# Sums of inner pieces made on GpSimd behind its own loads, in the second layer of a seven-product feed-forward

## What is computed

```python
hn = rms_norm(h, p['norm_ff_g'])
ff = jnp.square(jax.nn.relu(hn @ p['w_ff1'])) @ p['w_ff2']
return h + ff
```

## Time and profile before

| | us |
|---|---|
| median of 3 runs (lowest to highest) | 2295.55 (2292.86 to 2296.75) |
| profiled execution, its own time | 2294.14 |
| its span, first to last instruction | 2292.3 |
| TensorE busy / VectorE / ScalarE / GpSimd | 2216.3 / 1443.3 / 1068.5 / 166.5 |
| mean granted TensorE clock | 0.991 |

### The profile page before, as it was taken

How to read it: one execution, slowest core, us unless ns; L and a number is a source line. 1 busy time by engine, 2 the same in 40 slices (tenths; PEclk the granted TensorE clock), 3 DMA queues, 4 the chain that set the end, 5 groups by cost and what they waited for, 6 DMA issues and landing times.

```text
span 2292.3 us, 35228 instructions
## 1 busy us (share of the span) xinstructions
PE 2216.3 (97%) x13706; PEld 1996.7 (87%) x13706; DVE 1443.3 (63%) x2196; ACT 1068.5 (47%) x1870; POOL 166.5 (7%) x284
## 2 busy tenths in 40 slices
PE   8999999899998999999899999999999998899998
PEld 6888888788886888888688888999999998899998
DVE  6332455476654666677677554567677686766677
ACT  7533322265664444576634233465555643344432
POOL 0000000211100000000000000011111111111110
PEclk9999999999999999999999999999999999999999
DMA  5334322654546677888764344545546578887886
GB/s 167 108 110 138 119 93 74 164 137 131 146 122 173 227 231 242 254 260 269 248 234 125 89 160 144 175 162 197 205 161 222 168 274 307 260 253 245 271 308 212
DMA packets 227980, 434.92 MB, mean 190 GB/s; under 512 B 16355, under 2 KB 132963, under 8 KB 223116
## 3 DMA queue, kind: packets, MB, share of 16 engines
q1 hardware_dynamic: 188652, 321.71, 43.5%
q0 software_dynamic: 39200, 111.45, 15.6%
HBM read 331.93 MB, written 103.27 MB: 190 GB/s over the span
## 4 chain that ended last, share of the span: by engine, by line
PE 40%; DVE 7%; ACT 3%; issue 0%; DMA 0%; ACTq 0%; DVEq 0%
PE acc L148 11%; PE acc L150 11%; PE acc L149 11%; PE late_acc L148 2%; PE late_acc L149 2%; PE late_acc L150 2%; DVE w_lo L2535 2%; ACT ff_far_t_hi L2462 1%; DVE ff_far_t_lo L2540 1%; ACT w_hi L2465 1%; DVE ff_w_s L2589 1%; DVE ff_part_q L2593 1%; DVE ff_part_v L2593 1%; DVE t_lo L2540 1%; ACT t_hi L2462 1%
## 5 line engine op out<-in xcount | busy, mean ns | idle before, releaser
L148 PE MATMUL acc<-xn_hi,w_hi 128*128 128x512 f32 (+1 forms) x1176 | 420.6, 358 | 23.1 <-DVE xn_lo L617 10.0
L149 PE MATMUL acc<-xn_hi,w_lo 128*128 128x512 f32 (+1 forms) x1176 | 418.1, 356 | 0.0
L150 PE MATMUL acc<-xn_lo,w_hi 128*128 128x512 f32 (+1 forms) x1176 | 417.5, 355 | 0.0
L148 PE MATMUL late_acc<-xn_hi,w_hi 128*128 128x512 f32 (+1 forms) x768 | 285.9, 372 | 3.0 <-DVE late_result_a L867 1.9
L148 PEld LDWEIGHTS acc<-xn_hi,w_hi 128*128 128x128 f32 x1176 | 223.4, 190 | 58.1 <-issue 13.6
L150 PE MATMUL late_acc<-xn_lo,w_hi 128*128 128x512 f32 (+1 forms) x768 | 273.5, 356 | 0.0
L149 PE MATMUL late_acc<-xn_hi,w_lo 128*128 128x512 f32 (+1 forms) x768 | 272.8, 355 | 0.0
L150 PEld LDWEIGHTS acc<-xn_lo,w_hi 128*128 128x128 f32 x1176 | 223.2, 190 | 31.6
L149 PEld LDWEIGHTS acc<-xn_hi,w_lo 128*128 128x128 f32 x1176 | 223.4, 190 | 31.1
L149 PE MATMUL acc<-ff_far_t_hi,w_lo 128*128 128x320 f32 x804 | 249.7, 311 | 0.0
L148 PE MATMUL acc<-ff_far_t_hi,w_hi 128*128 128x320 f32 x540 | 168.4, 312 | 12.4 <-ACT hn_plain L2490 8.2
(11 more groups left out here) (312 smaller groups left out, 4609.4 us busy)
## 6 DMA issues: line engine op xcount, KB each, us to landing
w_raw<-in_w_tiles SPq DMA_DIRECT2D x82, 512.0 KB, 4.2
ff_w_s<-in_w_ff SPq DMA_DIRECT2D x64, 512.0 KB, 5.2
gates<-s_t_ops POOLq DMA_DIRECT2D x86, 320.0 KB, 3.6
ff_part_q<-s_u_T POOLq DMA_DIRECT2D x34, 640.0 KB, 5.9
c_w<-s_ac SPq DMA_DIRECT2D x20, 1024.0 KB, 5.0
ff_part_v<-s_u_T POOLq DMA_DIRECT2D x31, 640.0 KB, 5.5
s_late_T<-late_result_s SPq DMA_DIRECT2D x20, 640.0 KB, 7.1
ff_w_a<-in_w_ff SPq DMA_DIRECT2D x12, 1024.0 KB, 5.9
```

Source lines behind the costliest of these rows:

```text
L148: pe.matmul(out, w_hi, x_hi, start=first, stop=False, skip_group_check=onto)
L149: pe.matmul(out, w_lo, x_hi, start=False, stop=False, skip_group_check=onto)
L150: return pe.matmul(out, w_hi, x_lo, start=False, stop=last, skip_group_check=onto)
```

## The change

The sums of two inner pieces in the second layer are made by GpSimd instead of VectorE: behind the issue of the load for piece n, GpSimd waits for the load of piece n - 2 and adds its two pieces. VectorE keeps the sums of weights and makes them for the step after the next instead of the next, and in the second layer it makes the low half of the inner piece before that of the weights. Waits, counts and buffers are the same otherwise.

```diff
--- before.py
+++ after.py
@@ -2313,6 +2313,15 @@
                 at = self.INNER[i]
                 pool.wait_ge((out.even_out, out.odd_out, out.odd_out, out.mixed_out)[min(at, 3)], 16 * (k + 1))
             pool.dma_start(self.t_raw[s], self.t_ops[self.INNER[i], k]).then_inc(self.t_in[s], 16)
+
+        def add_pieces(n):
+            _, _, _, t, t_op, t_turned, _ = self.PRODUCTS[n // self.PAIRS]
+            r, H = n % self.RING, self.HALF
+            if len(t) == 2:
+                pool.wait_ge(self.t_in2[r], 16 * (n // self.RING + 1))
+                x, y = self.t_raw2[r][:, 0:H], self.t_raw2[r][:, H:2 * H]
+                pool.tensor_tensor(x, y if t_turned else x, x if t_turned else y, t_op).then_inc(self.t_sum2, 1)
+
         for n in range(self.STEPS - self.FIRST):
             p, r = n % self.PAIRS, n % self.RING
             pieces = self.PRODUCTS[n // self.PAIRS][3]
@@ -2334,6 +2343,10 @@
                 pool.dma_start(self.t_raw2[r].rearrange("p (q t) -> p q t", q=2), self.u_T[p, :, lo:hi + 1:hi - lo]).then_inc(self.t_in2[r], 16)
             else:
                 pool.dma_start(self.t_raw2[r][:, 0:self.HALF], self.u_T[p, :, pieces[0]]).then_inc(self.t_in2[r], 16)
+            if n >= 2:
+                add_pieces(n - 2)
+        for n in (self.STEPS - self.FIRST - 2, self.STEPS - self.FIRST - 1):
+            add_pieces(n)
 
     def sync(self, sp):
         ws, m, H, out = self.ws, self.m, self.HALF, self.out
@@ -2581,16 +2594,12 @@
             dve.scalar_tensor_tensor(at, at, 0.0, self.root[:, H * (q % 2):H * (q % 2 + 1)], ALU.max, ALU.mult).then_inc(self.relued, 1)
 
         def add_pieces(n):
-            w, w_op, w_turned, t, t_op, t_turned, _ = self.PRODUCTS[(n - self.FIRST) // self.PAIRS]
+            w, w_op, w_turned = self.PRODUCTS[(n - self.FIRST) // self.PAIRS][0:3]
             r, loaded = (n - self.FIRST) % self.RING, 16 * ((n - self.FIRST) // self.RING + 1)
             if len(w) == 2:
                 dve.wait_ge(self.w_in2[r], loaded)
                 x, y = self.w_raw2[r][:, 0:512], self.w_raw2[r][:, 512:1024]
                 dve.tensor_tensor(x, y if w_turned else x, x if w_turned else y, w_op).then_inc(self.w_sum2, 1)
-            if len(t) == 2:
-                dve.wait_ge(self.t_in2[r], loaded)
-                x, y = self.t_raw2[r][:, 0:H], self.t_raw2[r][:, H:2 * H]
-                dve.tensor_tensor(x, y if t_turned else x, x if t_turned else y, t_op).then_inc(self.t_sum2, 1)
 
         def add_result(p, c, f, of, cols):
             mh, th, op = self.PRODUCTS[p][6][c]
@@ -2619,12 +2628,12 @@
                     dve.tensor_tensor(self.a21[:, k], self.a11[:, k], self.a21[:, k], ALU.subtract).then_inc(self.s_sum, 1)
                 self.remainder_t(dve, n)
             else:
+                self.remainder_t(dve, n)
                 self.remainder_w(dve, n)
-                self.remainder_t(dve, n)
             if n == 3:
                 self.out.mix(dve, 3)
-            if self.FIRST <= n + 1 < self.STEPS:
-                add_pieces(n + 1)
+            if self.FIRST <= n + 2 < self.STEPS:
+                add_pieces(n + 2)
             for f in range(4):
                 if n >= 7 + f:
                     ended = self.ends(n, self.RING - 1 + f)
```

## The result

The changed kernel takes 2298.74 us (median of 20 runs, 2295.22 to 2301.60), the kernel before 2294.88 beside it (20 runs, 2290.34 to 2296.75): a ratio of 1.0016, 95% interval [1.0009, 1.0023]. That is no change by the 0.2% of the prediction, with a slowdown of 0.1 to 0.2% behind it; the forecast was 2280. The profiled spans are 2295.0 and 2292.3 us. Of all runs here one, out of the four of experiment 9, took 2329.42 us at a mean granted clock of 0.912 instead of 0.99, and it is left out of that experiment's numbers.

What follows compares the result with a forecast made beforehand. TensorE was taken to bound the kernel, losing about 24 us to waits on VectorE and ScalarE and a slower clock; gains 0.7 + 8.1 + 3.6 + 3.1 = 15.5 off 2294.14, plus 1.4 for the median, gave 2280, range 2267 to 2294.

Steps and rivals of the forecast that it cites:

- the ceiling of 24 to 25 us: Second layer, products 1, 2, 3 and 7: their excess over 56.4 us each, the most the change can touch.
- the ring: VectorE and ScalarE waiting on each other each step in product 2: 4.15 us a turn, 0.63 over TensorE's step.
- The sum taken as 1.5 us: Assumed length of one GpSimd sum of inner pieces, chosen between ends of 0.74 and 2.3 us.
- In turns: Assumption that GpSimd's sum and VectorE's two-operand SBUF instructions never overlap; most likely case, 2274 to 2287, chance 0.50.
- the rival at 2271: GpSimd's sums run fully beside VectorE's instructions, so all of 24 to 25 us goes; chance 0.28.
- a step of products 1, 2 and 7 costs 1.95 + 1.5 = 3.45: VectorE's own 1.95 us a step plus GpSimd's sum, without a result added; under TensorE's 3.52.
- its gain of 8.1: Border into product 2: TensorE's wait of 7.15 and 1.5 of slow clock go, less a rest of 0.5 us.
- product 7's 3.1: Into and inside product 7: gain of 1.1 for the border wait plus 2.0 us inside.
- Into product 1: Border before product 1: three VectorE steps and two sums take 11.1 us instead of 12.5, gain 0.7; clock still falls.
- Into product 3: Border before product 3: wait falls from 5.74 to about 3 us, plus 0.9 inside product 2; gain 3.6.
- the rival "no change": A sum near 2.0 us in turns, or later loads, cancels the gain: 2290 to 2300 us, chance 0.10.
- the signs named: Timeline marks for right (under 1 us idle before product 2, sums 1.3 to 1.7) or wrong (waits inside products over 0.7).

Runs made afterwards that it cites:

- experiment 9: Kernel before with both sums on VectorE two steps ahead, low halves swapped, GpSimd making only the 32 sums of products 3 and 6: 2271.17 us, ratio 0.9899.
- Experiment 1: Changed kernel with the 80 sums of inner pieces back on VectorE, still two steps ahead, low halves swapped: 2267.70 us, ratio to before 0.9889.
- experiment 8: Kernel before with only the sums made two steps ahead, all on VectorE, low halves in the old order: 2269.08 us, ratio 0.9897.
- experiment 2: Changed kernel with GpSimd zeroing the second piece (a write, no read) in place of the sum: 2268.0 us, one run.
- experiment 3: Changed kernel with GpSimd summing only 320 of the 640 columns: 2272.74 us, one run.
- experiment 5: Changed kernel with GpSimd making the sum for piece n - 2 ahead of the load of piece n: 2280.59 us, ratio 0.9945.

## Why the prediction was wrong, point by point

- **What bounds the kernel, and the ceiling of 24 to 25 us: right.** Experiment 1 gives back 24.4 by the rest.
- **Sums two steps ahead open the ring and cost nothing: right** (experiment 8). **"Swapping the two low halves moves nothing": wrong.** Alone it gives 1171.7 - 1149.7 = 22 us. I asked only whether TensorE needs both halves, not which of ScalarE's two high halves VectorE waits for first.
- **80 sums off VectorE: right as a count**, but once the ring is open the room is worth only 0.8 us (experiment 2).
- **The sum taken as 1.5 us: near**, 1.59 measured. **In turns, not beside each other: right**; the rival at 2271 fell.
- **The step that failed: "in turns, a step of products 1, 2 and 7 costs 1.95 + 1.5 = 3.45".** It charged VectorE the sum's length. Measured is 3.77, and 4.50 with a result instead of 4.19; products 3 and 6 take 3.32 and 4.05 instead of 2.85 and 3.59. VectorE loses 1.83 us at a sum in product 2 and 1.96 in product 3 (a t_lo of 2.78 beside a sum of 1.57): the sum's length, and 0.2 to 0.4 us ahead of its record, in which VectorE's instruction already stands. Of the 0.33 us too little, 0.09 is the sum itself and 0.24 this time ahead of it. The forecast 3.45 lay 0.07 under TensorE's step; 3.77 lies 0.25 over it. With so thin a margin, 0.3 us a step decided the sign of product 2 (experiment 3, with 1.13 lost a sum, has no wait there): its gain of 8.1 became none (a wait of 3.31, a clock of 0.70 behind it, and waits inside for the low half), and product 7's 3.1 a loss of 4.2.
- **Into product 1: a gain of 0.7 forecast, 6.4 lost.** I let the two engines alternate. The trace shows one instruction held for 4.75 us through two sums, and later steps of 4.65 where 4.19 was costed.
- **Into product 3: 3.6 forecast (0.9 of it inside product 2), 6.6 gained, and not for the reason given.** Its border wait is gone and the clock stays at 1.00, but ScalarE's copy comes no sooner: it starts 880.4 us into the rest, against 879.7 before (1998.81 and 2000.20 in the profiles). TensorE comes later, since it waited in products 1 and 2. Products 1 to 3 together take 190.8 us in both kernels, where the forecast had gained 12.4; product 7's loss of 4.2 is nearly all of the difference.
- **What came true was the rival "no change", "a sum near 2.0 us in turns", 2290 to 2300**, at 0.10: by its time and by what VectorE loses at a sum, mostly 1.8 to 2.0, not by the sum's own length. The text had the point from which it decides, 0.3 us a sum over 80 sums; what it lacked was a reason to put VectorE's loss above the sum's own length.
- **Of the signs named:** the ring of 4.15 is gone, the sums lie in 1.3 to 1.7, VectorE's instructions are longer just where a sum runs; against it, 3.31 instead of under 1 us before product 2, and waits over 0.7 inside products 2 and 7.

The net: the reordering gave 24.4 us, the move to GpSimd took 29.3, by the rest of the profiles; 4.8 slower, of which the timed medians show 3.9.

## What to carry to other kernels

Before work is moved to an idle engine, ask what the move holds up on the busy one: here a sum that costs VectorE 0.70 us to make cost it 1.67 us when GpSimd made it right behind a load's issue, and 0.97 when the sum mostly had to wait first. Split a change with two parts, a reordering and a move, and time each alone: all of the gain lay in the reordering, and either half of it was enough. Where a ring of two engines paces a kernel, look first for the order in which the waiting engine needs only the first of the other's results.

## What the runs showed of the hardware

- A GpSimd instruction that reads SBUF and a VectorE instruction with two SBUF operands run one behind the other, whole instructions at a time. In the changed kernel a VectorE instruction begun 0.10 to 0.53 us ahead of the sum's record stood until the sum's end, with only 0.11 to 0.13 us of its own length done; beside half sums and copies the pattern is the same (1.13 us lost at 0.89, 0.90 at 0.73). The Trainium skill, SBUF — State Buffer, section "Who interferes with whom", has these two share a read interface, and not one that only writes; the runs agree on both (2.51 beside a sum, 0.68 beside a write). That section's rule that whoever issues first keeps what is shared (stated there for other VectorE modes) fits experiment 5, where VectorE's instruction went first in all 54 cases; it fits the changed kernel only if a sum that follows another GpSimd instruction at once counts as issued before its record begins, which no run here shows.
- The wait goes both ways: a sum that starts while VectorE's instruction is under way lasted 1.83 instead of 1.58 us, and up to 2.27 (experiment 5).
- A held instruction is not let in between two sums, even over the time in which GpSimd issues a load: 4.75 us in the changed kernel over an issue of 0.72, 4.21 in product 1 over one of 0.56, and 4.03 in product 7 through two sums with nothing between them.
